# Query blocks 6 and 7 computed as a seventeenth pair of the projection, and prompt attention filled with gate products alone

## The reference

```
h    = rms_norm(x, g_pre_mix)
proj = h @ w_in                      # 1024 x 5120: [u_a | v_a | q | k | v_b], 1024 columns each
... spatial gating of u_a and v_a gives y_a; stick-breaking attention of q, k, v_b gives y_b
gates  = sigmoid(h @ w_gate + b_gate)          # 1024 x 2048: [g_a | g_b]
merged = g_a * (y_a @ w_branch_a) + g_b * (y_b @ w_branch_b)
x = x + rms_norm(merged @ w_o, g_post_mix)
... then the conv FFN with its own norms
```

## Time and profile before

| | |
|---|---|
| median of 3 runs | 2139.41 us (2137.74 to 2140.78) |
| the profiled execution | 2138.59 us, span 2136.8 us |
| PE | 2070.1 us busy (97%), 13704 matmuls |
| DVE, ACT, POOL | 66%, 45%, 35% |
| projection | 0 to about 505.6 us of the span |
| prompt attention | 505.6 to about 935 us |
| mean granted clock of PE | 0.994 |

### The profile page before, as it was taken

How to read it: one execution, slowest core, us unless ns; L and a number is a source line. 1 busy time by engine, 2 the same in 40 slices (tenths; PEclk the granted TensorE clock), 3 DMA queues, 4 the chain that set the end, 5 groups by cost and what they waited for, 6 DMA issues and landing times. The chain is left out here.

```text
span 2136.8 us, 35593 instructions
## 1 busy us (share of the span) xinstructions
PE 2070.1 (97%) x13704; PEld 1953.3 (91%) x13704; DVE 1419.5 (66%) x2242; ACT 958.1 (45%) x1773; POOL 742.8 (35%) x499
## 2 busy tenths in 40 slices
PE   5999999998999999999999999999999999999998
PEld 5998999998899999998999978899999999988875
DVE  5956544443787788857556557598888888834565
ACT  4334534433777777754342122243333333423343
POOL 2333355554644454436565210003333334100000
PEclk9999999999999999999999999999999999999999
DMA  5434344768546555546666433311222222563654
GB/s 175 116 98 133 131 166 166 206 187 238 150 120 144 125 131 142 136 149 176 190 183 205 157 126 99 89 61 61 72 74 79 67 86 62 194 206 127 217 183 163
DMA packets 313278, 298.65 MB, mean 140 GB/s; under 512 B 51767, under 2 KB 275991, under 8 KB 313111
## 3 DMA queue, kind: packets, MB, share of 16 engines
q1 hardware_dynamic: 299776, 265.61, 42.8%
q10 hardware_dynamic: 11094, 22.65, 2.9%
q0 software_dynamic: 2240, 8.13, 1.0%
HBM read 210.03 MB, written 86.30 MB: 139 GB/s over the span
## 5 line engine op out<-in xcount | busy, mean ns | idle before, releaser
L1786 DVE TENSOR_TENSOR_SCAN p_rest<-p_rest 128x896 f32<-128x896 f32 (+7 forms) x128 | 215.0, 1692 | 78.4 <-ACT p_rest L1705 78.4
L1555 POOL TENSOR_TENSOR p_weights<-p_weights,p_rest 128x895 f32<-128x895 f32 (+7 forms) x128 | 162.4, 1275 | 202.6 <-DVE p_rest L1786 202.6
L3355 DVE TENSOR_TENSOR p_w_lo<-p_w_raw,p_w_hi 128x512 fp32r<-128x512 f32 (+1 forms) x168 | 161.0, 963 | 54.4 <-ACT p_w_hi L3147 54.3
L3147 ACT ACTIVATE p_w_hi<-p_w_raw 128x512 fp32r<-128x512 f32 (+1 forms) x186 | 139.3, 772 | 68.0 <-DVE p_rows L3374 37.0
L172 PE MATMUL p_psB<-hT_lo,w_hi 128*128 128x274 f32 (+2 forms) x528 | 161.4, 306 | 4.2 <-issue 2.4
L174 PE MATMUL p_psB<-hT_hi,w_lo 128*128 128x274 f32 (+2 forms) x528 | 159.2, 302 | 0.0
L173 PE MATMUL p_psB<-hT_hi,w_hi 128*128 128x274 f32 (+2 forms) x528 | 159.1, 301 | 0.0
L172 PE MATMUL ps_up<-mergedT_lo,p_w_hi 128*128 128x274 f32 (+1 forms) x488 | 149.2, 306 | 4.1 <-DVE p_rows L3438 1.7
L1130 DVE TENSOR_TENSOR p_x<-p_psB,p_x 128x274 f32<-128x274 f32 (+1 forms) x168 | 70.6, 436 | 118.8 <-PE p_psB L174 113.0
L174 PE MATMUL ps_up<-mergedT_hi,p_w_lo 128*128 128x274 f32 (+1 forms) x488 | 148.4, 304 | 0.0
L173 PE MATMUL ps_up<-mergedT_hi,p_w_hi 128*128 128x274 f32 (+1 forms) x488 | 148.3, 304 | 0.0
(11 more groups left out here) (456 smaller groups left out, 7053.1 us busy)
## 6 DMA issues: line engine op xcount, KB each, us to landing
p_w_raw<-in_w_down SPq DMA_DIRECT2D x66, 512.0 KB, 3.8
p_w_raw<-in_w_up SPq DMA_DIRECT2D x44, 512.0 KB, 5.1
hid_scratch<-p_rows ACTq DMA_DIRECT2D x22, 545.0 KB, 2.9
p_raw_more<-in_w_in SPq DMA_DIRECT2D x20, 512.0 KB, 5.2
w_raw<-in_w_in SPq DMA_DIRECT2D x20, 512.0 KB, 5.3
p_kT<-k_hi_scratch SPq DMA_DIRECT2D x32, 256.0 KB, 4.7
p_kT<-k_lo_scratch SPq DMA_DIRECT2D x32, 256.0 KB, 5.2
w_raw<-in_w_gate SPq DMA_DIRECT2D x16, 512.0 KB, 5.0
```

The costliest lines, as they stand in the source:

```text
L1555: nc.gpsimd.tensor_tensor(wt[:, b % 6, 0:n - 1], wt[:, b % 6, 0:n - 1], rest[:, b % 4, 1:n], ALU.mult).then_inc(s("weights"), 1)
L1786: nc.vector.tensor_tensor_scan(src, src, src, 1.0, ALU.mult, ALU.bypass).then_inc(s("scanned"), 1)
L3147: nc.scalar.activation(target(w_hi, key), source(key), ACT.Copy).then_inc(s("w_hi"), 1)
L3355: nc.vector.tensor_tensor(target(w_lo, key), source(key), target(w_hi, key).bitcast(F32), ALU.subtract).then_inc(s("built"), 1)
```

## The change

`Q_FIRST` becomes 8, so the projection has 40 blocks and 17 pairs, and the last pair is query blocks 6 and 7. The block that opens the next phase and the one loaded after it are gate blocks 0 and 1. The raw weights of gate block 1 go to a buffer that the last pair uses, so their load waits until that pair's weights are built and is issued by SP after the stores of the pair before. The product S4 of the last pair takes the place of S3 (the plain split of the opening block needs the place it would have had), so ACT waits for the end of product S3 before it builds S4's high part.

In prompt attention the filling is 14 blocks of gates (1008 matmuls, of which 891 are dealt to the 96 units by the same shares); `q_take`, `q_lo` and `store_q` are gone.

```diff
-Q_FIRST = 6
+Q_FIRST = 8
...
     def place(q, j):
+        if (q, STEPS[j]) == (PAIRED - 1, "S4"):
+            j = STEPS.index("S3")
         return (2 * (SLOTS - 1) + NS * q + j) % OPS
...
         def raw(n):
+            if n == NB + 1:
+                return w_raw[:, 0, :]
...
                     elif n >= RAW + PLAIN:
-                        built(sp, pair_of(n - RAW), NS - 1)
-                        built(sp, pair_of(n - RAW), STEPS.index("S3"))
+                        user = PAIRED - 1 if n > NB else pair_of(n - RAW)
+                        built(sp, user, NS - 1)
+                        built(sp, user, STEPS.index("S3"))
...
                     if q < PAIRED - 1:
                         load(n + 4)
-                        load(n + 5)
+                        if n + 5 < NB:
+                            load(n + 5)
...
+                load(NB + 1)
                 store(NB - 2)
                 store(NB - 1)
...
                     at = NS * q + j
-                    if at >= OPS:
+                    if (q, step) == (PAIRED - 1, "S4"):
+                        act.wait_ge(s("prod"), 2 * (NS * q + STEPS.index("S3")) + 2)
+                    elif at >= OPS:
                         act.wait_ge(s("prod"), 2 * (at - OPS) + 2)
...
-    QB = KT - Q_FIRST
-    NQ = NCH * QB
-    DB = QB + G_FIRST
+    DB = G_FIRST
     NE = NCH * DB
...
                 load_kq(0)
-                store_q(0)
                 load_v(0)
-                store_q(1)
                 load_w(2)
                 load_kq(1)
                 load_v(1)
+                store_gate(0)
+                store_gate(1)
                 for k, (w, g) in enumerate(UNITS):
                     for e in range(max(groups_ended(k - 1), 2), groups_ended(k)):
-                        if e < NQ:
-                            store_q(e)
-                        else:
-                            store_gate(e)
+                        store_gate(e)
...
                 split(1)
-                for e in range(2):
-                    q_lo(e)
                 for b in range(2 * LEAD):
                     weigh(b)
-                    if b % 2:
-                        q_lo(2 + b // 2)
                 split(2)
                 for k in range(len(UNITS)):
-                    for e in range(groups_ended(k - 1) if k else groups_ended(0), min(groups_ended(k), NQ)):
-                        q_lo(e)
                     for b in scored(k):
                         weigh(b)
```

More of the change, by code:

```diff
@@ L489, in columns @@
                 def columns(n):
-                    at = FROM[KINDS[n]] + n % KT * P if n < NB else FROM["Q"] + (Q_FIRST + n - NB) * P
+                    if n >= NB:
+                        return a["w_gate"][0].rearrange("(k p) c -> p k c", p=P)[:, :, gate_columns(n - NB)]
+                    at = FROM[KINDS[n]] + n % KT * P
                     return w_in[:, :, at:at + P]
@@ L1408, in gate_units @@
     def gate_units(b):
-        return len(range(b, NE - NQ, GST))
+        return len(range(b, NE, GST))
     with ExitStack() as ctx:
@@ L1444, in load_kq @@
                     b, p, at = h % 2, h // 2, DH * (h % 2)
-                    if p >= Q_FIRST:
-                        for half in range(2):
-                            sp.wait_ge(s(f"q_stored{half}"), 32 * ((NCH * (p - Q_FIRST + 1) + 1 - half) // 2))
                     if h >= 2:
@@ L1465, in load_w @@
                 def load_w(n):
-                    if n < QB:
-                        src = w_in[:, :, 2 * D + (Q_FIRST + n) * P:2 * D + (Q_FIRST + n + 1) * P]
-                    else:
-                        src = w_gate[:, :, gate_columns(n - QB)]
-                    ring.load(sp, n, (n + 1) % 2, src, KT)
+                    ring.load(sp, n, (n + 1) % 2, w_gate[:, :, gate_columns(n)], KT)
                 def load_w_ahead(n):
@@ L1475, in load_w_ahead @@
                     sp.dma_start(ring.raw[:, (n + 1) % 2, :].rearrange("p (k c) -> p k c", k=KT),
-                                 w_gate[:, :, gate_columns(n - QB)]).then_inc(kept("w_ahead"), 16)
+                                 w_gate[:, :, gate_columns(n)]).then_inc(kept("w_ahead"), 16)
                 def load_ya(j):
-                    for b in range(2):
-                        sp.wait_ge(s(f"q_stored{b}"), 32 * ((NQ + 1 - b) // 2))
                     sp.dma_start(stage[:, j, :], d.ya[j]).then_inc(kept(f"ya_ready{j}"), 16)
@@ L1486, in load_raw_k @@
                     sp.dma_start(raw_k[:], k_past[:, :, 0:P]).then_inc(kept("raw_k_ahead"), 16)
[L1488 to L1493, removed]
                 def store_gate(e):
-                    g, c, b = e // NCH - QB, e % NCH, (e - NQ) % GST
+                    g, c, b = e // NCH, e % NCH, e % GST
                     sp.wait_ge(s("emptied"), e + 1)
@@ L1567, in rest_of @@
                                             ALU.subtract).then_inc(ring.split, 1)
[L1569 to L1573, removed]
                 ring.start_pool(pool, 1)
@@ L1718, in gate @@
                 def gate(e):
-                    g, b = e // NCH - QB, (e - NQ) % GST
+                    g, b = e // NCH, e % GST
                     bias = PAR["b_gate"] + g
                     act.wait_ge(s("group"), e + 1)
-                    if e - NQ >= GST:
-                        act.wait_ge(kept(f"gate_stored{b}"), 16 * ((e - NQ) // GST))
+                    if e >= GST:
+                        act.wait_ge(kept(f"gate_stored{b}"), 16 * (e // GST))
                     nc.scalar.activation(gates[:, b, :], psD[e % 3][:, 0:CH], ACT.Sigmoid,
                                          bias=par[:, bias:bias + 1]).then_inc(s("emptied"), 1)
[L1727 to L1740, removed]
                 def y_low_rows(w):
@@ L1760, in _ @@
                 for e in range(2):
-                    empty(e)
+                    gate(e)
                 for b in range(2 * LEAD):
@@ L1764, in _ @@
                     if b % 2:
-                        empty(2 + b // 2)
+                        gate(2 + b // 2)
                 for k, (w, g) in enumerate(UNITS):
```

## The result

The changed kernel takes 2145.0 us (median of 10 runs, 2142.43 to 2146.77) against 2137.7 for the kernel before on the same chip: ratio 1.0031, 95% interval 1.0022 to 1.0041. It is slower by about 7 us, above the forecast range, which ended at 2144.2. The other 0.9 lies around the span: 2.1 to 3.0 us in the ten runs of the changed kernel and 1.8 before. No row shows what it is.

A forecast was written before the change was run, and what follows sets the result against it. The prediction took PE, busy in 97% of the span, to bound the kernel. Its terms, +21.2 - 23.8 + 4.8 - 3.2 = -1.0 us, gave a median of 2138.4 us, range 2132.9 to 2144.2.

The forecast's parts named there:

- The pair: End of the projection: a seventeenth pair of Q blocks adds 168 matmuls, +21.2 us.
- S4's wait: Last projection pair: S4's high part waits for the end of S3; cost 0, at most 0.5 us if DVE is late.
- The filling: Attention: 144 matmuls of 364 columns leave, at 0.1656 us each, -23.8 us if PE were bound by its own work.
- The start: First heads of attention: without query chunks in ACT's and POOL's queues, PE's waits there shrink, -3.2 us.
- What PE does not get back: +4.8: Unit A's transposes of tile 7: filling removed after tile 7's scores in E brings nothing, 0.32 us a head, 15 heads.
- The output sum: Next place in a head where PE meets DVE: 1.0 us of room, of which the change takes about 0.3.
- Costed at 0: End of the projection: the later load of gate block 1 is hidden by the closing 12 us, cost 0.
- For the keys I kept 0: Start of attention: PE's wait of 3.41 us for the keys left unchanged, 0 in the sum; bounds 0 and 4.5.
- the rule on pipelined descriptors: Key loads: value loads following at once overlap their tail and could put the keys a little later; counted 0.
- DVE and ACT set the whole head: Slower rival, attention heads: fewer matmuls leave the head at 24.8 us; 2155.9 in full, mostly 2144 to 2150; chance 0.13.
- the turning point: Attention heads: the loss a head from which the slower rival decides against the change, 0.67 us.
- PE gets it all back: Faster rival, attention heads: tile 7's chain shortens as much as the filling without `q_take` and `q_lo`; 2134.4 us; chance 0.17.

The follow-up runs named there:

- experiments 4: Kernel before with filling shares A, B 11, C 15, D 11, E 12, F 12, more of it behind tile 7's scores: 2134.65 us, ratio 0.9987.
- experiment 5: Changed kernel plus six idle matmuls of 256 columns at the end of unit F of each head from the second on: 2143.13 us, ratio 1.0031.
- Experiment 7: Changed kernel plus 13 idle matmuls a head, spread over units A to F, from the second head on: 2156.05 us, ratio 1.0084.
- 11: Kernel before with shares A, B 11, C 15, D 11, E 12, F 12 and gate weights 3 loaded ahead of the fifth query store: 2132.1 us, ratio 0.9981.
- 12: Changed kernel with tile 7's multiplication split in two, gate block 1 loaded earlier, shares A 11, B 12, C 14, D 11, E 12, F 12: 2126.07 us, ratio 0.9953.
- Experiment 1: Changed kernel with gate block 1 loaded before the quarter of hT is brought back, not after the stores: 2142.97 us, ratio 1.0031.
- experiment 10: Kernel before with POOL's multiplication of tile 7 in two instructions, keys 0 to 511 first: 2131.34 us, ratio 0.9975.
- experiment 9: Changed kernel with POOL's multiplication of tile 7 in two instructions, keys 0 to 511 first: 2128.86 us, ratio 0.9967.

## Why the prediction was wrong

**What held.** The pair: 21.21 us, and S4's wait cost nothing, since attention opens 21.0 us later. The filling: a matmul less is 0.1656 us less wherever nothing binds (units B, C, D, F). The start: of the first head's -4.8, 1.5 are its filling, so 3.3 came from ACT's and POOL's queues, 3.2 predicted. The order of time of the mechanism: PE is bound at A's transposes by tile 7, in all 15 heads.

**The step that failed** is "What PE does not get back: +4.8", which let the chain begin at tile 7's scores in E. It measures 14 x 0.69 + 1.3 for the last head's A = 10.9 us. The place of the wait was right and the start of the chain was not: it begins one tile earlier, at tile 6's scores in D.

- *The chain runs through tile 6.* I dated tile 7's scan by the start of its row. But that row can hold a wait. Where no POOL instruction runs beside it, a scan of 1024 takes 2.29 us (one scan each in experiments 4, 5, 7, 11 and 12; this is number 5):

```profile
547.37 2.29 DVE L1751 TENSOR_TENSOR_SCAN p_rest<-p_rest 128x1024 f32<-128x1024 f32 x1 [1.87 <-ACT p_rest L1685]
```

In the heads of both kernels it starts while POOL still multiplies tile 6, and it ends 2.14 to 2.15 us after POOL's end, however early it starts. The head of the earlier trace rows, where tile 6's mask product and multiplication are

```profile
701.43 0.28 PE L1621 MATMUL p_psZ<-p_mask,p_unit 128*128 128x256 f32 x1
...
704.45 1.78 POOL L1555 TENSOR_TENSOR p_weights<-p_weights,p_rest 128x895 f32<-128x895 f32 x1 [3.90 <-DVE p_rest L1786]
```

has 705.66 + 2.71 - 706.23 = 2.14; the head of the changed kernel above has 697.27 - 695.12 = 2.15; and one of its long scans, 673.49 - 671.35 = 2.14:

```profile
669.58 1.77 POOL L1545 TENSOR_TENSOR p_weights<-p_weights,p_rest 128x895 f32<-128x895 f32 x1 [1.96 <-DVE p_rest L1749]
...
670.26 3.23 DVE L1749 TENSOR_TENSOR_SCAN p_rest<-p_rest 128x1024 f32<-128x1024 f32 x1
```

The Trainium skill, "SBUF — State Buffer", section "SBUF: two separate sides", says that DVE with two SBUF inputs and GpSimd take one port pair in turn, for a whole instruction. The heads agree: between the last two the scan starts 0.56 us earlier against POOL's end, and its row is 0.55 us longer.

So the chain is tile 6's mask product, sigmoid, scan and multiplication, then tile 7's scan and multiplication. From that mask product to PE's first transpose of tile 7 it is 9.06 to 9.08 us in 11 of the 15 heads before and in 10 of the 15 after. Counted from tile 7's mask product, the same heads give 5.58 to 5.79 us before and 5.75 to 5.94 after, so that part seems to grow only because PE comes to tile 7's scores sooner; the mean scan of tile 7, 2.66 us before and 2.86 after, grows with it. In the stretch from tile 6's mask product PE has 22.7 filling matmuls before and 19.2 after, in the mean of 14 heads: 3.5 x 0.1656 = 0.58 us were taken out there, and none of it comes back. My sum had 0.28 to 0.36. Experiment 7 fits the longer chain better. Of its 13 idle products a head, 7 lie outside this stretch, 7 x 0.118 = 0.83 us; 9 lie outside the one from tile 7's scores, 1.06 us; a head became longer by 0.76.

- *The chain is longer in some heads.* In 5 of the 15 heads it takes 9.6 to 10.6 us, in 4 of them while POOL still splits gate weights when tile 6's scan starts. Before, it was longer in 4. Over the 14 heads the mean went from 9.18 to 9.29 us. Counted from one first transpose of tile 7 to the next, a head went from 25.00 to 24.24 us and lost 0.73 of 1.49: the 0.58, these 0.11, and 0.04 elsewhere. The wait inside the eight transposes, 0.30 us a head before, is 0.81 after.

- *The output sum.* I saw 1.0 us of room at one head and let the change take 0.3 of it. It doesn't have that room in every head: PE waits for `y_sum` in 7 places, up to 0.5 us, in E (0.14 a head lost) and in A (0.05). What E loses lies inside the 9.07 us and would else have been waited for at the transposes. The DVE sum stands behind the long scans in DVE's queue.

**Costed at 0, measured 1.7 in one execution.** I wrote that the closing 12 us hide the load of gate block 1 and asked only when its result is wanted. It is not late for POOL. But it is issued at 514.73 and lands after 11.1 us, and the last query stores, which the keys' loads wait for, share the DMA engines with it: the last lands after 5.7 us instead of 4.2. Experiment 1 shows it in the keys' loads, not in the total. In experiment 10, where no such load stands there, the last store also takes 5.8 us, so the size of this term is not shown.

**The rest.** The forecast of 2138.4 stood on a median of 2139.4 from three runs; ten give 2137.7, so as a change the miss is larger, +7.3 instead of -1.0. The 1.2 us gained after attention beyond the plan I can't name; between experiments 10 and 9 the same stretch is 1.6 us longer, so it is within the scatter of single executions. For the keys I kept 0: from the load's issue to the first score it is 9.46 us before, 9.86 in the changed kernel and 9.37 in experiment 1, and 9.34 to 9.86 in all traces. So the rule on pipelined descriptors that I weighed there (the Trainium skill, "DMA: Bandwidth & Descriptors", section "Two DMAs through the same engine are not ordered") is neither shown nor excluded. One reading of mine was off: before, the eight transposes take 0.86 to 1.68 us and not 0.87 to 1.1, and a head takes 25.06 in the mean of 14 and not the 24.80 of the one that I took as steady.

**The rivals.** "DVE and ACT set the whole head", mostly in part, named 2144 to 2150 and as the turning point 0.67 us lost a head; 2145.0 and 0.69 came, but its reason was wrong, since in experiment 9 the same DVE and ACT work fits into 23.33 us. It is a latency at one place and not a throughput. "PE gets it all back" was wrong in that the chain doesn't shorten with `q_lo` and `q_take` gone (9.07 us in most heads of both kernels, longer in the mean). Once the chain was cut, 1.32 of the 1.49 us did come back.

## What to carry to other kernels

Taking work off the busiest engine pays only where no other engine's result is awaited before the work's end; find every such place in the loop and follow its chain back until it starts at work of the busiest engine itself. A row that is longer than the same instruction elsewhere may hold a wait, as the scan did, and then the chain goes on behind it. Here a wait of 0.28 us, hidden in the length of a row, stood for 11 us that never came back. Once such a wait is found, look at what the waiting instruction really needs: half of the tile was enough, and that edit alone was worth 0.0064 x 2137 = 13.7 us. Test a chain's start over many heads: counted from the right one its length stays the same when the pace changes.

## What the runs showed of the hardware

DVE's scan of 1024 takes 2.29 us with POOL idle and up to 3.24 where it starts beside a POOL multiplication; it then ends 2.14 to 2.15 us after that. A POOL multiplication of 1023 takes 2.00 and the two halves 1.10 and 1.21, in sum 0.31 more. And the clock: before attention PE stands idle for 2.76 us in the changed kernel and 1.94 in the one before, and in the 3.4 us behind it the mean granted clock is 0.63 of full in the one, because from 527.6 on it is at the lower level of 1.2 GHz (0.50), and 1.00, the level of 2.4 GHz, in the other. The length of the idle time does not decide it alone: in experiment 5, with 2.94 us idle at the same place, the clock stays at 1.00. The changed kernel, the one before and experiment 5:

```profile
526.60:530.00 3.40, 3.38 (x14) 3.40 (x15) 0.00 (x0) 0.00 (x0) 1.74 (x5) 0.63 0.81 320
```

```profile
505.60:509.00 3.40, 3.36 (x20) 3.39 (x21) 0.00 (x0) 0.00 (x0) 1.76 (x5) 1.00 0.67 261
```

```profile
525.10:528.50 3.40, 3.37 (x20) 3.40 (x21) 0.00 (x0) 0.00 (x0) 1.75 (x5) 1.00 0.80 316
```

14 matmuls instead of 20 in that time cost about 1 us, and nothing in the end as far as the rows tell, because PE then waits 3.67 us for the keys.
